# A layer's first gating product ahead of the branch rows' transposes, and products that begin with the leading turned piece

## What is computed

```python
xn = modulate(rms_norm_2(h, g_norm_mix[l]), sh1, sc1)
p = xn @ w_in[l]                       # keys, values, queries, z, and 3 x 1024 gate columns
y_a = diff_post(diff_attention_latent(...), da_subln_g[l], lam_init)   # rms_norm by head
y_b = spatial_gating(...)
y_c = neighbourhood_attention(...)
...
def merge_branches(p_gate, y_a, y_b, y_c, w_branch, w_out):
    yb = einsum('bnie,ied->bnid', stack([y_a, y_b, y_c]), w_branch)
    g = sigmoid(p_gate)
    return sum(g * yb, axis=2) @ w_out
```

## Time and profile before

| | us |
|---|---|
| median of 3 runs | 3637.53 |
| lowest, highest | 3635.95, 3638.95 |
| the profiled execution, its device time | 3640.39 |
| span of its trace | 3638.8 |
| mean granted TensorE clock | 0.892 of full |

### The profile page before, as it was taken

How to read it: one execution, slowest core, us unless ns; L and a number is a source line. 1 busy time by engine, 2 the same in 40 slices (tenths; PEclk the granted TensorE clock), 3 DMA queues, 4 the chain that set the end, 5 groups by cost and what they waited for, 6 DMA issues and landing times.

```text
span 3638.8 us, 35236 instructions
## 1 busy us (share of the span) xinstructions
PE 2825.0 (78%) x13005; PEld 1786.3 (49%) x13005; DVE 1311.0 (36%) x2532; ACT 763.0 (21%) x973; POOL 1032.2 (28%) x495
## 2 busy tenths in 40 slices
PE   4879889997995986889865887773697885787774
PEld 2658667676873764566651222221584562222221
DVE  2732233344216226632352222223527243222223
ACT  0323322233421113411101111111124210111111
POOL 0067656633862331132201000001262530000000
PEclk8989999998996997889977999997799987989997
DMA  7565468852552441122317999997141556999997
GB/s 287 171 203 185 146 207 282 281 184 68 185 177 87 145 158 45 37 82 91 118 58 269 374 374 373 375 377 282 68 129 49 171 196 217 372 374 373 374 376 260
DMA packets 366107, 780.62 MB, mean 215 GB/s; under 512 B 15076, under 2 KB 16274, under 8 KB 365216
## 3 DMA queue, kind: packets, MB, share of 16 engines
q1 hardware_dynamic: 337312, 669.61, 52.8%
q0 software_dynamic: 28672, 109.36, 8.8%
HBM read 733.58 MB, written 62.62 MB: 219 GB/s over the span
## 4 chain that ended last, share of the span: by engine, by line
PE 54%; DMA 16%; DVE 14%; SPq 6%; issue 6%; ACT 2%; POOL 2%; POOLq 0%; DVEq 0%; ACTq 0%
PE banks L707 10%; PE banks L708 10%; PE banks L712 10%; PE banks L1041 5%; PE banks L733 5%; PE banks L1063 4%; SPq L579 4%; DMA tokens_out<-in_moe_w_up 3%; DMA arena<-moe_x 2%; DMA weight_ring<-in_moe_w_up 2%; DMA weights_high<-in_moe_w_down 2%; SPq L587 2%; DMA weight_ring<-in_dil_w_qkv 2%; PE banks L783 1%; DMA rel_rows<-arena 1%
## 5 line engine op out<-in xcount | busy, mean ns | idle before, releaser
L1521 POOL TENSOR_TENSOR weight_ring_r<-weight_ring,weights_high_r 128x2048 fp32r<-128x2048 f32 x124 | 563.9, 4554 | 643.3 <-ACT weights_high_r L1271 448.7
L707 PE MATMUL banks<-weights_high_r,x_transposed_r 128*128 128x512 f32 x1216 | 494.6, 407 | 49.2 <-DVE x_transposed_r L1764 12.3
L1271 ACT ACTIVATE weights_high_r<-weight_ring 128x2048 fp32r<-128x2048 f32 x124 | 234.2, 1898 | 868.9 <-PE banks L712 509.8
L712 PE MATMUL banks<-weight_ring_r,x_transposed_r 128*128 128x512 f32 x1600 | 390.7, 390 | 5.3 <-POOL weight_ring_r L1521 5.2
L712 PEld LDWEIGHTS banks<-weight_ring_r,x_transposed_r 128*128 128x128 f32 x1600 | 299.2, 188 | 72.6 <-POOL weight_ring_r L1521 10.7
L1653 POOL DMA_DIRECT2D moe_y<-arena x64 | 33.8, 529 | 1034.2 <-DVE arena L2261 1000.4
L1521 POOL TENSOR_TENSOR weight_ring_r<-weight_ring,gates_r 128x2048 fp32r<-128x2048 f32 (+1 forms) x60 | 271.0, 4527 | 151.4 <-DVE small L1715 79.9
L707 PEld LDWEIGHTS banks<-weights_high_r,x_transposed_r 128*128 128x128 f32 x1216 | 236.1, 194 | 118.3 <-issue 26.2
L1041 PE MATMUL banks<-weight_ring,arena 128*64 128x512 f32 x1024 | 247.6, 616 | 53.8 <-DMA weight_ring<-in_moe_w_up 32.1
L783 PE MATMUL banks<-constants,scaled_rows 128*128 128x128 f32 x594 | 102.8, 335 | 209.6 <-DVE scaled_rows L1774 174.7
L2243 DVE TENSOR_TENSOR arena<-banks,arena 64x1024 f32<-64x1024 f32 x64 | 77.9, 1217 | 368.6 <-ACT arena L1395 368.6
(11 more groups left out here) (333 smaller groups left out, 4365.1 us busy)
## 6 DMA issues: line engine op xcount, KB each, us to landing
weight_ring<-in_moe_w_gate SPq DMA_DIRECT2D x64, 1024.0 KB, 15.7
weight_ring<-in_moe_w_up SPq DMA_DIRECT2D x64, 1024.0 KB, 15.2
weights_high<-in_moe_w_down SPq DMA_DIRECT2D x64, 1024.0 KB, 16.1
x_transposed<-in_moe_w_gate SPq DMA_DIRECT2D x60, 1024.0 KB, 16.1
tokens_out<-in_moe_w_up SPq DMA_DIRECT2D x60, 1024.0 KB, 15.4
arena<-in_moe_w_down SPq DMA_DIRECT2D x60, 1024.0 KB, 16.2
weight_ring<-in_w_in SPq DMA_DIRECT2D x56, 1024.0 KB, 5.2
weight_ring<-in_w_ada SPq DMA_DIRECT2D x48, 1024.0 KB, 7.2
```

The lines of the kernel that those rows point to most:

```text
L707: nc.tensor.matmul(banks[t][:, 0:width], xh, wh[:, k, :], start=k0 + k == 0, stop=False)
L712: last = nc.tensor.matmul(banks[t][:, 0:width], lhs(k0 + k, t)[0], wl[:, k, :], start=False, stop=k0 + k == g.k_tiles - 1)
L1271: nc.scalar.activation(high(s, kn, width), slot(c, kn, width), ACT.Copy).then_inc(high_ready, 1)
L1521: nc.gpsimd.tensor_tensor(slot(c, kn, width, ring_r), slot(c, kn, width), high(s, kn, width), ALU.subtract).then_inc(low_ready, 1)
```

## The change

- `first_chunk` is a new order for the first chunk of a product whose rows have just been turned. TensorE doesn't wait for all pieces; tile by tile it waits for one turned piece and runs the high matmuls of that tile and weight group. All high matmuls of both groups come first, then the low ones by group. It holds for `g_o`, `g_ff_in`, `g_ple_g` of both layers of the first block, for `g_dil`, and for `g_kv` and `g_out` of both layers of the second.
- `gate_ahead` runs the first gating product of a layer directly behind `neighbourhood`, ahead of the branch rows' transposes. Its matmuls with `xh` (against `wh` and `wl`) come first, the ones with `xl` last, behind the wait for `low_back`.
- GpSimd makes the low parts of this product's weights behind its last mask, and issues the return of `x_low` before the gates' transfer. The broadcast row is loaded before the attention, and VectorE asks for it there.
- VectorE copies the first gating product's banks before the turned branch rows.
- The transpose of ada columns stands in front of `turn_rows`, and VectorE's copy of it at the start of the layer.

```diff
+            def first_chunk(g, lhs, turned):
+                width = g.chunks[0][1]
+                split = g.first_split[0]
+                banks = [acc_bank() for _ in range(g.tiles)]
+                for t in range(g.tiles):
+                    for i, (k0, kn) in enumerate(g.groups):
+                        pe.wait_ge(high_ready, split + i + 1)
+                        pe.wait_ge(tr_used, turned[t, k0 // 4])
+                        wh = high(split + i, kn, width)
+                        for k in range(kn):
+                            xh, xl = lhs(k0 + k, t)
+                            nc.tensor.matmul(banks[t][:, 0:width], xh, wh[:, k, :], start=k0 + k == 0, stop=False)
+                            nc.tensor.matmul(banks[t][:, 0:width], xl, wh[:, k, :], start=False, stop=False)
+                for i, (k0, kn) in enumerate(g.groups):
+                    pe.wait_ge(low_ready, split + i + 1)
+                    wl = slot(chunk[0], kn, width, ring_r)
+                    chunk[0] += 1
+                    for t in range(g.tiles):
+                        for k in range(kn):
+                            last = nc.tensor.matmul(banks[t][:, 0:width], lhs(k0 + k, t)[0], wl[:, k, :],
+                                                    start=False, stop=k0 + k == g.k_tiles - 1)
...
+            def gate_ahead(g, lhs, layer):
...
+                for i, (k0, kn) in enumerate(g.groups):
+                    pe.wait_ge(high_ready, split + i + 1)
+                    pe.wait_ge(low_ready, split + i + 1)
+                    wh, wl = high(split + i, kn, width), slot(chunk[0] + i, kn, width, ring_r)
+                    for t in range(g.tiles):
+                        for k in range(kn):
+                            xh = lhs(k0 + k, t)[0]
+                            nc.tensor.matmul(banks[t][:, 0:width], xh, wh[:, k, :], start=k0 + k == 0, stop=False)
+                            nc.tensor.matmul(banks[t][:, 0:width], xh, wl[:, k, :], start=False, stop=False)
+                pe.wait_ge(low_back, 16 * (layer + 1))
+                for i, (k0, kn) in enumerate(g.groups):
...  (matmuls of lhs(k0 + k, t)[1] with wh; acc_ready per tile, w_used after the first group)
@@ TensorE, close_block; the same for g_ple_g, g_dil, g_kv, g_out
-                turn_rows(LT)
-                copied()
-                product(g_o, two_split)
+                turned = turn_rows(LT)
+                product(g_o, two_split, turned=turned)
@@ TensorE, a layer of the second block
-                turn_rows(MAX_TILES)
-                copied()
                 pe.wait_ge(src_ready, seen.next(src_ready))
                 a = i * ADA_W + 8 * KD
                 transposes([ada[:, a:a + 4 * KD]], m=4 * KD)
-                product(g_kv[i], x_early, turn_chunk(MAX_TILES, lambda n: n in (0, 2)))
+                turned = turn_rows(MAX_TILES)
+                product(g_kv[i], x_early, turn_chunk(MAX_TILES, lambda n: n in (0, 2)), turned)
...
                 neighbourhood(i)
+                gate_ahead(g_gate[i][0], x_late, i)
                 for t in range(tiles):
                     for b in range(3):
                         pe.wait_ge(src_ready, seen.next(src_ready))
                         transposes([ar((YA, U, YC)[b] + t * 512 + j * P, P) for j in range(4)])
                 copied()
-                pe.wait_ge(low_back, 16 * (i + 1))
                 for n in range(6):
                     b = n % 3
-                    product(g_gate[i][n], x_late)
+                    if n > 0:
+                        product(g_gate[i][n], x_late)
@@ GpSimd
                 for k in range(4):
                     mask_bias(k)
+                row(I["da_subln_g_2"][layer], P)
...
+                low_parts(g_gate[layer][0])
                 pool.wait_ge(na_out, base + len(na_steps(layer)))
+                nc.gpsimd.dma_start(A_r[:, XL:XL + KD * MAX_TILES * P], low_dram).then_inc(low_back, 16)
                 pool.wait_ge(scratch_out, 16 * (DEPTH + DIL_G + layer + 1))
                 nc.gpsimd.dma_start(GT[:, :], gate_dram[layer].partition_broadcast(P)).then_inc(gates_in, 16)
-                nc.gpsimd.dma_start(A_r[:, XL:XL + KD * MAX_TILES * P], low_dram).then_inc(low_back, 16)
-                row(I["da_subln_g_2"][layer], P)
                 after_turn()
-                low_parts(g_gate[layer][0])
@@ VectorE
                 say(misc_ask)
+                say(src_ready)
+                v(copy(gate_rows[...], turned_bank()[0:4 * KD, 0:P]), tr_used)
...
+                say(misc_ask)
                 dve.wait_ge(low_saved, 16 * (layer + 1))
                 attention(diff_units(layer))
                 neighbourhood(layer)
-                say(misc_ask)
...
-                for t in range(tiles):
-                    for b in range(3):
-                        ... copy_turned(dst[:, b * 4:b * 4 + 4, t, :])
                 for n in range(6):
                     half, b = n // 3, n % 3
                     for t in range(tiles):
                         bank = product_bank()
                         v(copy(ar(MERGED_SIG + t * 512, BANK), bank[:, :]), acc_used)
                         say(act_req)
+                    for t in range(tiles if n == 0 else 0):
+                        ... copy_turned(dst[:, k * 4:k * 4 + 4, t, :]) for k in range(3)
```

More of the change, by code:

```diff
@@ new lines, in gate_ahead @@
+            def gate_ahead(g, lhs, layer):
+                width = g.chunks[0][1]
+                split = g.first_split[0]
+                banks = [acc_bank() for _ in range(g.tiles)]
+                for i, (k0, kn) in enumerate(g.groups):
[9 more added lines that the diff above has]
+                for i, (k0, kn) in enumerate(g.groups):
+                    wh = high(split + i, kn, width)
+                    for t in range(g.tiles):
+                        for k in range(kn):
+                            last = nc.tensor.matmul(banks[t][:, 0:width], lhs(k0 + k, t)[1], wh[:, k, :],
+                                                    start=False, stop=k0 + k == g.k_tiles - 1)
+                        if k0 + kn == g.k_tiles:
+                            last.then_inc(acc_ready, 1)
+                    if k0 + kn < g.k_tiles:
+                        last.then_inc(w_used, 1)
+                chunk[0] += len(g.groups)
@@ L720, in product_chunk @@
+            def product_chunk(g, n, lhs, turned=None):
+                if turned is not None:
+                    first_chunk(g, lhs, turned)
+                    return
                 col, width = g.chunks[n]
@@ L738, in product_chunk, with product @@
                         last.then_inc(w_used, 1)
-            def product(g, lhs, after=None):
+            def product(g, lhs, after=None, turned=None):
                 done = []
@@ L752, in product @@
                 for n in range(len(g.chunks)):
-                    product_chunk(g, n, lhs)
+                    product_chunk(g, n, lhs, turned if n == 0 else None)
                     done.append(made.now(acc_ready))
@@ L786, in turn_rows @@
             def turn_rows(tiles, k_tiles=KD):
+                turned = {}
                 for t in range(tiles):
@@ L791, in turn_rows @@
                         transposes([rows(t)[:, j * P:(j + 1) * P] for j in range(k, min(k + 4, k_tiles))])
+                        turned[t, k // 4] = made.now(tr_ready)
+                return turned
             def turn_chunk(tiles, wanted):
@@ L1163, in turn_hidden @@
                                 for k in range(2) for t in range(LT)])
-                product(g_ff_in[i], two_split, turn_hidden)
+                product(g_ff_in[i], two_split, turn_hidden, turned)
                 copied()
@@ L1174, in _ @@
             close_block(0, g_mla_o)
-            turn_rows(LT)
-            copied()
-            product(g_dil, two_split, turn_chunk(LT, lambda n: n % 6 < 4))
+            turned = turn_rows(LT)
+            product(g_dil, two_split, turn_chunk(LT, lambda n: n % 6 < 4), turned)
             dilated()
@@ L2318, in _ @@
                 say(misc_ask)
+                say(src_ready)
+                v(copy(gate_rows[0:4 * KD, layer * P:(layer + 1) * P], turned_bank()[0:4 * KD, 0:P]), tr_used)
                 loaded()
```

30 lines of the change are left out of this document (15 added, 15 removed).

## The result

The changed kernel takes 3574.08 us, median of 4 runs (3568.82 to 3581.94), beside 3637.47 (3635.95 to 3638.95, 4 runs) for the kernel before on the same chip: ratio 0.9828, 95% interval 0.9808 to 0.9847, 63 us less. The profiled execution is the longest of the four, 3581.94 us with a span of 3580.2. Two later measurements on other chips, each with 5 runs, gave medians of 3571.49 and 3577.68; so medians of one kernel lie some 6 us apart from one series to the next, and small differences are only read within one series or in the traces.

The account below looks back on a forecast made before the run. TensorE, busy for 78% of the span, was taken as the bound, with time won where it idles. Terms 21 + 16 + 19 + 12 = 68 us off gave 3572, and 3569.5 us as median; range 3554 to 3594.

Parts of the forecast that it names:

- Gating product first, layer 0: Behind layer 0's attention: gating product covers VectorE's work, branch product starts at 1571.9 instead of 1593.2; 21 us, bounds 18 to 22.
- The same, layer 1: Gating product behind layer 1's attention, x_low slightly late: branch product at 2835.6, not 2851.4; 16 us, bounds 12 to 17.
- First chunk of four tiles: kv of both layers and out of layer 0, started by turned pieces: 9, 8 and 2 us, together 19, bounds 12 to 23.
- First chunk of two tiles: Eight two-tile products, where GpSimd sets the end: 1.5 us each, together 12 us, bounds 6 to 16.
- the second low group waits for 454.06 and ends at 455.9: 1.5 us: Block 0's gate product: second low group waits for GpSimd's subtractions; chunk ends at 455.9 instead of near 457.4.
- Empty first chunks: Rival: first chunks give nothing, gains go into waits for subtractions and VectorE; 37 us left, 3600 us; 12%.
- Early subtractions that stall the attention: Rival: two subtractions of 4.57 us per layer stall the neighbourhood attention; 18 us go, 3588 us; 8%.
- More than the sum: Rival: VectorE stays ahead of subtractions in following chunks, so stalls like that at 2607 us go too; 3551 us; 8%.
- Slower: Rival: fresh stalls of 4.97 us in all 16 kv and qz chunks cost 80 us; 3649 us; 2%.
- nothing arrives: Rival: the experts wait for DMA, which ran ahead before, so the gain is lost; 3637 us; 3%.
- the row that the forecast left open: Trace at 2607 us, which could not show whether VectorE gets in between two GpSimd subtractions; no size given.

Follow-up runs that it names:

- the kernel with the earlier GpSimd: Changed kernel with GpSimd released after the last row copy, not the last turned copy, in turns without gain: 3548.88 us, ratio 0.9773.
- The experiment with the multiplications first: Changed kernel with the multiplications of g_out's gated rows before their sums with the residual, in both layers: 3571.99 us, ratio 0.9827.

## Why the prediction was right, and where its terms were off

The forecast was 3569.5 us, the measurement 3574.08: the mechanism holds, and the sum is 63 instead of 68 us. Part of the agreement is luck: in the profile the two-tile products and the gating product of layer 1 gave some 10 us less than forecast and kv of layer 0 gave 5.3 more, of which 3.9 come from the clock in the attention.

- **Gating product first, layer 0**: 21 forecast, 21.5 at the first branch product's start. That product takes 15.5 us instead of 13.9 in this trace, where the clock falls behind a wait of 2.18 us for the turned copies; 19.9 are left. The wait has the same length in every kernel with the gating product first, the clock doesn't follow every time: the product takes 14.0 us in three traces, 15.4 to 15.5 in eight and 17.1 in one.
- **The same, layer 1**: mis-sized, 16 forecast. The attention's end to the branch product shrank by 13.3 us, and 1.8 more were lost in the slower branch product. The forecast had x_low late by 1.4 us; it was late by 1.9, since GpSimd issued it 1.8 us after the attention's end (2769.28) and not 0.6: its second subtraction ended at 2769.91, and then it needed 1.16 us more. What had no term is the clock: the third part was put at 3.6 us and took 5.52. Here too executions differ; in the kernel with the earlier GpSimd the clock stays at 1.00 behind the same wait:

```profile
2751.11 3.94 PE L765 MATMUL banks<-weights_high_r,arena_r 128*128 128x512 f32 x16 [1.94 <-DMA arena_r<-x_low]
```

- **First chunk of four tiles**: kv of layer 0 won 9.9 us in its own chunk, 9 forecast; the other 4.4 us of its row are 3.9 of the clock in the attention, as said, and 0.5 on the way there. Kv of layer 1 won 8.9, 8 forecast. The prediction's remark that in kv GpSimd is done 4 us before it is needed holds for the old order (1182.6 against 1186.96); by its own new times it is 2.8 and 1.8 us, and in the trace of the changed kernel 1.7 and 0.8. No wait came of it. Out won 5.6 by the end of its first chunk and lost all of it to the stretched sums. The forecast took 2 of bounds 0 and 4; the profile shows -0.5, just outside. The experiment with the multiplications first shows that the sums' place in the queue was the cause.
- **First chunk of two tiles**: mis-sized, 12 forecast, about 6 in the profile. It is the step "the second low group waits for 454.06 and ends at 455.9: 1.5 us". GpSimd's end was right, but the group that waits for it ran at 1.20 GHz there and took 1.65 us more, which is all that was won. Over all eight products the slower groups cost 6.3 us in this trace, the whole of what is missing. The lower bound of 6 was there for another reason (weights that come late). The earlier release of GpSimd removes wait and slow group together and wins 3.2 to 5.7 us in each of five products.
- **Rivals.** Empty first chunks: refuted, they give 30.5 us alone. Early subtractions that stall the attention: refuted by the unstretched rows under them, and by the stretch up to the attention's end: 165.3 us with the first chunks alone, where nothing is subtracted under it, and 165.2 to 165.4 in eight kernels with early subtractions (four more lie between 164.4 and 168.2, the kernel before at 168.3). As the Trainium skill has it (SBUF — State Buffer, Who interferes with whom), VectorE instructions with at most one SBUF input, outside its two-port modes, don't contend with GpSimd, and the trace agrees: copies out of a bank kept their 0.42 and 0.69 us. More than the sum: no; kv's second chunk in layer 1 has two stretched sums (4.15 and 2.90 us) where it had one (4.97). Slower and nothing arrives: refuted.

By the row that the forecast left open, whether VectorE gets in between two subtractions: it does. The first subtraction of 1778.14 ends at 1782.99 and the second at 1787.95, and the two waiting sums end at 1783.54 and 1788.49, each 0.5 us behind one of them. So the first sum was done while the second subtraction was already under way. The second takes 4.99 us instead of 4.57; the first takes 4.85, as a sum was still running when it began (1777.82 to 1778.51).

## What to carry to other kernels

Where work is pulled ahead of a wait, look for what it will wait for next, and price that wait with the slower matmuls that may follow it, as a range; here they took back the whole 1.5 us in the gate product of block 0 and nothing in the first of the eight products. When one engine's work becomes the end of a stage, its start condition is worth rereading: GpSimd waited for copies that it doesn't disturb, and releasing it a few microseconds earlier was worth 21 to 27 us more, a third of the whole change. A semaphore that frees a bank belongs behind an instruction that nothing stretches, but it only helps if the next bank's reader isn't queued behind the stretched one.

## What the runs showed of the hardware

- A wait of 2 us can be followed by some microseconds of TensorE at 1.20 GHz, but the length of the wait alone doesn't tell. After 2.40 us idle, up to 451.65 us, the clock was 0.52 over 3.5 us and eight matmuls took 3.63 us; after 2.38 us, up to 190.13 us, eight took 2.14 at the full clock. After 1.90 us it was 0.66 over 5 us, in another kernel after 1.94 us 1.00. Behind one and the same wait of 2.18 us a product of 32 matmuls took 14.0, 15.5 or 17.1 us. After 1.19 us at 447 us eight matmuls took 2.10 us, but after 1.06 us at 1016.9 us the clock was 0.66 over 5 us.
- A VectorE sum with all operands in SBUF that meets a running subtraction of GpSimd took 4.27 and 4.19 us instead of 0.69. Multiplications, copies and remainders with one operand in a bank kept 0.69 us under such subtractions.
- Two transfers of 2 MB issued 0.56 us apart by GpSimd landed after 7.4 and 11.9 us in the one order and 8.1 and 12.4 us in the other (layer 1), so here the first was favoured whatever it carried.
